# Split-precision products of a two-block transformer: three passes of 256 columns become one of 512 and one of 256

## The reference

```python
def swiglu(h, w_gate, w_up, w_down):
    return (jax.nn.silu(h @ w_gate) * (h @ w_up)) @ w_down

for l in range(2):
    x = x + 0.5 * swiglu(rms_norm(x, norm_g[l, 0]), ...)      # D_FF = 2816
    h = rms_norm(x, norm_g[l, 1])
    proj = h @ w_in[l]                                        # 3840 columns: q, k, v of three attentions
    ya, yb, yc = three attentions on the parts of proj
    g = sigmoid(h @ w_gate[l] + b_gate[l])
    x = x + (sum over the branches of g * (y @ w_branch)) @ w_o[l]
    x = x + 0.5 * swiglu(rms_norm(x, norm_g[l, 2]), ...)
```

## Time and profile before

| | |
|---|---|
| median of 3 executions | 2224.42 us (2220.97 to 2229.49) |
| the profiled execution | 2220.84 us, of it 2218.9 us span |
| TensorE busy | 2090.0 us (94%), 14045 matmul records |
| VectorE busy | 1187.9 us (54%) |
| ScalarE busy | 632.8 us (29%) |
| DMA | 471 MB, mean 212 GB/s |

### The profile page before, as it was taken

The page is one execution under the profiler, slowest core; times in us unless marked ns, Lnnn a source line. Parts: engine busy times, 40 slices in busy tenths (PEclk is TensorE's granted clock), DMA queues, the critical chain, the costliest instruction groups (busy, mean ns, idle before and its releaser), DMA issues.

```text
span 2218.9 us, 33949 instructions
## 1 busy us (share of the span) xinstructions
PE 2090.0 (94%) x14045; PEld 1694.3 (76%) x14045; DVE 1187.9 (54%) x2050; ACT 632.8 (29%) x934; POOL 0.2 (0%) x4
## 2 busy tenths in 40 slices
PE   7999999999999999999999999979893999999997
PEld 7999998779999999999878999968573444334443
DVE  6665658774655655666885555553556222222212
ACT  4433434423333533344441433320321000000000
POOL 0000000000000000000000000000000000000000
PEclk9999999999999999999999999989996999999999
DMA  7966552238866666654233676512321899999994
GB/s 227 281 204 181 169 166 84 86 114 225 263 211 195 196 212 204 181 171 152 67 114 106 229 234 210 164 39 76 133 103 69 333 416 416 415 416 415 416 417 186
DMA packets 287144, 471.36 MB, mean 212 GB/s; under 512 B 17306, under 2 KB 223188, under 8 KB 286988
## 3 DMA queue, kind: packets, MB, share of 16 engines
q1 hardware_dynamic: 285680, 466.19, 61.3%
q10 hardware_dynamic: 1308, 2.96, 0.5%
HBM read 467.96 MB, written 1.13 MB: 211 GB/s over the span
## 4 chain that ended last, share of the span: by engine, by line
PE 82%; DMA 10%; DVE 5%; ACT 1%; issue 1%; SPq 1%; DVEq 0%; ACTq 0%
PE ps L618 81%; DMA ring_zone<-in_moe_w_up_dram 5%; DMA ring_over<-in_moe_w_gate_dram 4%; DMA W<-in_ffn_w_gate_dram 1%; PE ps L903 1%; DVE QK L1838 1%; SPq L556 0%; PE ps L1038 0%; DVE hl L1564 0%; DVE hT L1616 0%; DVE WL L1553 0%; DVE xT L1571 0%; DMA PT<-in_norm_g_dram 0%; PE ps L1156 0%; ACT WH L1243 0%
## 5 line engine op out<-in xcount | busy, mean ns | idle before, releaser
L1553 DVE TENSOR_TENSOR WL<-W,WH 128x1024 fp32r<-128x1024 f32 x372 | 453.0, 1223 | 341.9 <-ACT WH L1243 341.9
L618 PE MATMUL ps<-hh,WH 128*128 128x256 f32 x2128 | 610.1, 287 | 12.2 <-DVE WL L1553 6.6
L618 PE MATMUL ps<-hh,WL 128*128 128x256 f32 x2128 | 601.5, 283 | 0.0
L618 PE MATMUL ps<-hl,WH 128*128 128x256 f32 x2128 | 601.4, 283 | 0.0
L1243 ACT ACTIVATE WH<-W 128x1024 fp32r<-128x1024 f32 x372 | 391.5, 1056 | 496.8 <-PE ps L618 472.6
L618 PEld LDWEIGHTS ps<-hh,WH 128*128 128x128 f32 x2128 | 403.0, 189 | 33.0 <-issue 30.1
L618 PEld LDWEIGHTS ps<-hl,WH 128*128 128x128 f32 x2128 | 402.8, 189 | 0.2
L618 PEld LDWEIGHTS ps<-hh,WL 128*128 128x128 f32 x2128 | 402.8, 189 | 0.0
L618 PE MATMUL ps<-ring_over,XT 128*64 128x512 f32 x896 | 204.7, 596 | 24.4 <-DMA ring_over<-in_moe_w_up_dram 13.3
L618 PE MATMUL ps<-hid_h,WH 128*128 128x256 f32 x704 | 202.9, 288 | 0.0
L618 PE MATMUL ps<-hid_h,WL 128*128 128x256 f32 x704 | 198.7, 282 | 0.0
(11 more groups left out here) (315 smaller groups left out, 2338.4 us busy)
## 6 DMA issues: line engine op xcount, KB each, us to landing
ring_over<-in_moe_w_gate_dram SPq DMA_DIRECT2D x128, 512.0 KB, 14.8
ring_zone<-in_moe_w_down_dram SPq DMA_DIRECT2D x128, 512.0 KB, 15.1
ring_over<-in_moe_w_up_dram SPq DMA_DIRECT2D x96, 512.0 KB, 15.4
W<-in_ffn_w_gate_dram SPq DMA_DIRECT2D x88, 512.0 KB, 5.0
W<-in_ffn_w_up_dram SPq DMA_DIRECT2D x88, 512.0 KB, 4.0
W<-in_ffn_w_down_dram SPq DMA_DIRECT2D x88, 512.0 KB, 3.7
W<-in_w_in_dram SPq DMA_DIRECT2D x78, 512.0 KB, 3.9
W<-in_w_gate_dram SPq DMA_DIRECT2D x48, 512.0 KB, 3.6
```

What stands on the lines that cost most here:

```text
L618: ins = nc.tensor.matmul(o, lhsT, rhs, start=start, stop=stop, skip_group_check=True, **kw)
L1553: v.tensor_tensor(low, W[:, i % RAW, :], high.bitcast(F32), ALU.subtract).then_inc(low_ready, 1)
```

## The change

Gate, up and w_in are now computed by `beside`, as two passes instead of three. The two parts of an operand lie side by side (`hhl`, `WHL`, `hid_hl`). The first pass is stationary low x moving high, 256 columns; the second is stationary high x both parts of the moving side, 512 columns: high x high adds to the first half of the bank, high x low goes to the second half. So a tile of 256 columns fills a whole bank, and a product of two tiles takes two turns, both begun ahead of its first pass (`two_banks`). VectorE adds the halves of each bank (`joined`, a tensor_reduce over pairs 256 columns apart) into `S`, then scales from SBUF. In w_in a one-column copy after the scaling signals `projection_ready`, on which the attention waits in place of the freed bank. The down products and `w_gate` keep `mm3`. In chunk 14 the passes with 128 moving columns become one of 128 and one of 256.

```diff
-        WH = sb("WH", [P, PAIRS, PIECE], FR)
-        WL = sb("WL", [P, PAIRS, PIECE], FR)
+        WHL = sb("WHL", [P, PAIRS, 2, PIECE], FR)
...
+            def beside(bank, stat, mov, start, stop, then=None, at=0):
+
+                n = mov.shape[2]
+                mm(bank[:, at:at + n], stat[:, 1], mov[:, 0], start, False)
+                mm(bank[:, at:at + 2 * n].rearrange("p (a n) -> p a n", a=2), stat[:, 0], mov, False, stop, then=then)
...
+            def two_banks():
+
+                banks = [begin()]
+                turns.step()
+                banks.append(begin())
+                turns.step()
+                return banks
+
+            def two_tiles(kind, h_wait=False):
+
+                banks = two_banks()
...
-                            mm3(bank[:, f * T:(f + 1) * T], at(w, j * 256 + f * P), h_at(k),
-                                half + f + j == 0, k == KD - 1, then=then if f and k == KD - 1 else None)
+                            beside(banks[f], at(w, j * 256 + f * P), h_at(k), k == 0, k == KD - 1,
+                                   then=work_ready if k == KD - 1 else None)
...
-                            dve_did(proj[{0: 3, 1: 9, 2: 14}[branch]])
+                            pe.wait_ge(proj_ready, 15 * l + {0: 3, 1: 9, 2: 14}[branch] + 1)
...
-                    act.wait_ge(work_free, turns.n + 1)
+                    act.wait_ge(gated, due(gated))
...
+            def joined(dst):
+
+                bank = take()
+                give(v.tensor_reduce(dst, bank.rearrange("p (a t) -> p t a", a=2), AX.X, ALU.add))
+
+            def scale_by_factor(a):
+
+                return v.tensor_tensor(by_two(a), by_two(a), factor_by_two(), ALU.mult)
+
             def ffn(l, i):
                 for b in range(FF_BLOCKS):
                     used(2)
                     if b == 0:
                         used(2)
+                    for f in range(2):
+                        joined(sg[:, b % 2, f * T:(f + 1) * T])
+                    given()
+                    if b == 0:
                         norm_factor()
-                    bank = take()
-                    give(v.tensor_tensor(by_two(sg[:, b % 2, :]), by_two(bank), factor_by_two(), ALU.mult))
+                    scale_by_factor(sg[:, b % 2, :]).then_inc(gated, 1)
                     if b:
                         used(2)
-                    bank = take()
-                    give(v.tensor_tensor(by_two(hid_f[:, b % 2, :]), by_two(bank), factor_by_two(), ALU.mult))
+                    for f in range(2):
+                        joined(hid_f[:, b % 2, f * T:(f + 1) * T])
                     given()
+                    link(scale_by_factor(hid_f[:, b % 2, :]))
...
                     if c == 0:
                         used(2)
                         norm_factor()
-                    bank = take()
...
+                    two = S[:, c % 2, :]
+                    if c == 14:
+                        joined(two[:, 0:T])
...
+                        for f in range(2):
+                            joined(two[:, f * T:(f + 1) * T])
+                        given()
...
+                            ins = v.scalar_tensor_tensor(out=QK[:, tile:tile + 2, :], in0=by_two(two), scalar=scale,
+                                                         in1=factor_by_two(), op0=ALU.mult, op1=ALU.mult)
+                    link(ins)
+                    v.tensor_copy(rt[:, 0, 0:1], eps[:, :]).then_inc(proj_ready, 1)
```

More of the change, by code:

```diff
@@ L399, in build @@
         p_ready = ev("probs_ready")
+        proj_ready = ev("projection_ready")
         gate_ready = ev("tanh_ready")
@@ L819, in _ @@
                 ffn(l, 0)
-                proj = {}
                 for c in range(15):
-                    bank = begin()
                     if c not in (4, 5, 10, 11, 14):
-                        two_tiles("w_in", bank, h_wait=c == 0, then=work_ready)
+                        two_tiles("w_in", h_wait=c == 0)
                     else:
+                        banks = two_banks()
                         for half in range(2):
@@ L832, in _ @@
                                 if c == 14:
[L833 to L834 removed]
+                                    beside(banks[0], at(w, j * 256), h_at(k), k == 0, end,
+                                           then=work_ready if end else None)
                                 for tt in range(TT):
[L836 to L838 removed]
+                                    if c == 14:
+                                        beside(banks[1], h_at(k, tt * P, P), at(w, j * 256 + P), k == 0 and tt == 0,
+                                               end, then=work_ready if end and tt else None, at=tt * T)
+                                    else:
+                                        beside(banks[tt], h_at(k, tt * P, P), at(w, j * 256, 256), k == 0, end,
+                                               then=work_ready if end else None)
                             done_pair()
[L840 removed]
                     if c == 0:
@@ L1769, in _ @@
                         link(v.tensor_copy(rstd_of[:, :], ps[:, 0, 0:TT]))
-                    if c in (4, 5, 10, 11):
-                        at = (c - 4) * 256 if c < 6 else 512 + (c - 10) * 256
+                    two = S[:, c % 2, :]
+                    if c == 14:
+                        joined(two[:, 0:T])
+                        given()
+                        v.tensor_tensor(QK[:, 20, :], two[:, 0:T], rstd[:, :], ALU.mult)
+                        v.tensor_tensor(QK[0:64, 21, :], two[64:128, 0:T], rstd[0:64, :], ALU.mult)
+                        v.tensor_tensor(QK[64:128, 21, :], two[0:64, 0:T], rstd[64:128, :], ALU.mult)
+                        bank = take()
+                        give(v.tensor_reduce(by_two(two[:, T:2 * T]),
+                                             bank.rearrange("p (t a n) -> p t n a", t=TT, a=2), AX.X, ALU.add))
+                        given()
@@ new lines, in _ @@
+                    else:
+                        for f in range(2):
+                            joined(two[:, f * T:(f + 1) * T])
+                        given()
+                        if c in (4, 5, 10, 11):
+                            at = (c - 4) * 256 if c < 6 else 512 + (c - 10) * 256
+                            for tt in range(TT):
+                                ins = v.tensor_scalar(V[:, tt, at:at + 256], two[:, tt * 256:(tt + 1) * 256],
+                                                      rstd_of[:, tt:tt + 1], None, ALU.mult)
+                        else:
+                            tile = {0: 0, 1: 2, 2: 4, 3: 6, 6: 8, 7: 10, 8: 12, 9: 14, 12: 16, 13: 18}[c]
+                            scale = HD ** -0.5 if c in (0, 1, 6, 7, 12, 13) else 1.0
+                            ins = v.scalar_tensor_tensor(out=QK[:, tile:tile + 2, :], in0=by_two(two), scalar=scale,
+                                                         in1=factor_by_two(), op0=ALU.mult, op1=ALU.mult)
```

66 lines of the change are left out of this document (24 added, 42 removed).

## The result

The changed kernel takes 2232.4 us, median of 20 runs (2226.9 to 2238.2), beside 2224.1 us for the kernel before, median of 20 runs: ratio 1.0037, 95% interval 1.0026 to 1.0047. That is 8 us slower where 14 us faster was forecast. It lies inside the range (2186 to 2236) and within the 0.5% that a measurement hardly tells from no change, but on the other side, and its interval leaves out no change. The profiled execution took 2230.26 us, 9.4 more than that of the kernel before.

What follows compares the result with a forecast made beforehand. TensorE, busy 94% of the span, was taken as the bound, with DMA loading experts in the last 500 us. From the profiled 2220.8 us, 43 saved and 29 lost to waits gave 2207 us; range 2186 to 2236.

Steps and rivals of the forecast that it cites:

- the 512 pass: Merged products on TensorE: a 512-column pass takes 215.8 ns, hiding the next weight load; 21.4 ns saved per triple, 40 us.
- a fixed cost: Rival on TensorE's pitch: every pass pays 12 ns, long or short, 512 columns take 225; 2224 us, chance 0.15.
- The two bounds given for a pair: TensorE's merged pair: 109 + 216 ns if the load cost nothing (61 us), 118.6 + 237.2 if columns set it (3 us).
- Columns: Rival on TensorE: the operand's path limits float32r streaming, so 512 columns take 237 ns; 2247 us, chance 0.14.
- Chunk 14: In w_in, 32 load-bound triples of 128 columns become pairs of 0.11 + 0.12 us; 3 us saved.
- Chunk 2 of w_in: TensorE waits for chunk 0's banks, freed behind the reciprocal: 5.5 us stall plus 2.5 for the clock, in two layers.
- First blocks: First block of each feed-forward stage: TensorE waits for gate's additions behind a fourth `rests`; 1.1 us, four times, 4 us.
- Bias tables: Ten blocks with bias tables: a table waits for up's banks, whose additions are late; 8 us lost.
- Split pieces: Where a late DMA already made TensorE wait for a split piece, VectorE's longer queue adds 1 us.
- VectorE hides: VectorE's additions, 0.69 us each, fit under TensorE in the steady state, busy near 1355 us; costed at nothing.
- The attention wait: Attention behind w_in waits for `projection_ready`, 1.4 us later on VectorE, while TensorE has 8 us of work; costed at nothing.
- the last stage: From 1716 us on, loading experts with DMA engines 94% busy: the last 500 us keep their length.

Runs made afterwards that it cites:

- The series: Only TensorE passes behind one another, the kernel's computation left out; float32r passes of 256, 384 and 512 columns came 0.1207, 0.1735 and 0.2273 us apart.
- join_first: The changed kernel with w_in's chunk 0 additions ahead of the reciprocal instead of behind it; 2215.6 us, 0.9957 of the kernel before.
- added_twice: The changed kernel with VectorE reading each bank of two parts a second time ahead of the addition; 2270.6 us, 1.0209 of the kernel before.

## Why the prediction was wrong

- **The step that failed** is the 512 pass, "one of 512, whose stream hides the next load (215.8, the nearest row with that stream)". It takes 230 ns. The reading behind it, that the 12 ns above 256 columns are the weight load and vanish behind a longer stream, had its evidence from plain float32, another type. The series show some 14 ns on every float32r pass. Saved per pair 5 to 6 ns, not 21.4; over 1872 pairs 9.5 to 11.6 us, not 40. This term alone is 28 to 31 us, more than the whole miss of 25.
- The rival "a fixed cost", at 0.15, was the right mechanism. It said 0.344 a pair and 2224 us; the pair is 0.3512, because the fixed part is 2 ns more in each pass, and the place of the operands adds some 3 ns. The two bounds given for a pair (325 to 355.8) hold it.
- Columns (0.14) came nearer in the pitch of a pair (0.355), and its 2247 is too slow, since its losses of 29 us were too many. It is refuted by 384 and 512 alone. The sign that it named, 231 ns for a 512 pass, was met within a nanosecond, by another cause.
- The figure of 518 cycles for 512 columns that the prediction took from the Trainium skill ("TensorE: Matmul & The Clock Gate", section "Back-to-back issue gap") is met by a record of plain float32, 512 cycles long (0.2157 us), and by bfloat16 (0.216), but not by float32r (0.2273).
- Chunk 14: 3 us forecast, 3.5 measured.
- Chunk 2 of w_in: 5.5 + 2.5 us forecast per layer, 5.06 + 2.2 to 2.4 measured. `join_first` shows its cause.
- First blocks: 1.1 us forecast, 0.60 measured. Two additions take 1.28 us, not 1.38. They begin at 31.28 in the first stage, just as up's last pass starts, and TensorE then still has the two products with `ones` (from 31.47, 0.59 us) to do before it needs a bank; the forecast took at most 0.3 us off for them.
- Bias tables: 8 us forecast, 1.2 seen, in the one block that also turns two parts of the modulation (900.88). Failed step: "gate's two reduces push it 1.4 us on". In the block at 88 us the last rests ahead of up's additions end at 99.62 and before them VectorE idles 1.65 us for ScalarE's rounding, so gate's reduces lie in idle time. Before the change too these rests ended 0.39 us ahead of up, not with it. With the change the additions free the banks 0.7 and 1.3 us after up, before the tables come to need them.
- Split pieces: 1 us forecast, 1.6 measured, of it 0.5 at the late DMA and 1.06 at 55.03, a place that the prediction didn't have. Nor did it have the 0.61 us for additions at 570.01.
- VectorE hides: right but for these two. Busy 1327.5 us (1355 forecast), additions 0.683 (0.69). `added_twice` shows how near the end of the cover is: 0.69 us more for each bank costs 38 us.
- The attention wait and the last stage: nothing, as forecast.

With the pair at 0.351 the prediction's own sum would have been 2220.8 - 9 - 3 + 29 = 2238; with the table waits right, 2231.

## What to carry to other kernels

Take a pass's pitch only from rows of its own operand type, and where length is what changes, measure two lengths: the slope is the stream, the rest is a price per pass, and only that rest is saved by merging. When turns of a shared buffer start to reach over less work, look at the one place where the freeing instruction stands behind a late result: moving the additions there was worth 12 us by the traces and 17 by the times, where all that the merged passes bring is 10 to 15. After any change of allocation, look at the pitch and at GB/s again before reading a difference of 0.3% as an effect of the code, and ask whether the kernel before would have gained by the same place: here its triples did.

## What was not expected of the hardware

- A float32r pass costs some 14 ns above its columns at the full clock (0.1207, 0.1735, 0.2273 us for 256, 384, 512 at one place), and nothing at 1.2 GHz (213 and 427 ns for 256 and 512). Plain float32 and bfloat16 show 2.5 ns.
- The pitch of such passes depends on where the operands lie: 0.3467 to 0.3537 us for the same pair, 0.2275 or 0.2333 for 512 columns alone, and in the kernel before 355.8 or 359.2 ns for a triple (means).
- 32 bytes' shift of the receiving buffers took the DMAs from 416 to 409 GB/s, 7 to 10 us in the experts' stage.
